# Attention's weighted values with the values as the standing operand, two heads on the two halves of the array's columns

## The reference, cut to what matters

```python
s = jnp.where(causal[None, None], s, -jnp.inf)
p = jax.nn.softmax(s, axis=-1).astype(v.dtype)
return jnp.einsum('bhqk,bkhd->bqhd', p, v)
...
o = o.transpose(1, 0, 2, 3, 4).reshape(B, S, N_HEADS * V_HEAD_DIM)
return o @ w_o
```

## Time and profile before

| what | value |
|---|---|
| median of three runs | 783.43 us (783.41 to 783.67) |
| span of the profiled execution | 780.1 us |
| lies around the span, by the median | 3.3 us |
| PE busy | 773.0 us, 99% of the span |
| DVE busy | 577.1 us, 74% |
| ACT busy | 423.9 us, 54% |
| POOL busy | 97.7 us, 13% |
| the chain that ended last | 98% PE |
| granted clock of TensorE, mean | 0.998 |

### The profile page before, as it was taken

How to read it: one execution, slowest core, us unless ns; L and a number is a source line. 1 busy time by engine, 2 the same in 40 slices (tenths; PEclk the granted TensorE clock), 3 DMA queues, 4 the chain that set the end, 5 groups by cost and what they waited for, 6 DMA issues and landing times.

```text
span 780.1 us, 10183 instructions
## 1 busy us (share of the span) xinstructions
PE 773.0 (99%) x3678; PEld 652.6 (84%) x3678; DVE 577.1 (74%) x843; ACT 423.9 (54%) x601; POOL 97.7 (13%) x147
## 2 busy tenths in 40 slices
PE   9999999999999999999999999999999999999997
PEld 7998888888888888888889888888888888888885
DVE  6699999889675566655476999998877765457543
ACT  6577555664554355454475765564536544536441
POOL 2634000221300000000211240002304000000000
PEclk9999999999999999999999999999999999999999
DMA  9687545556566666676455784456564766667741
GB/s 356 239 287 227 192 162 158 194 164 199 182 237 217 210 198 223 217 238 210 128 199 169 247 270 162 134 173 206 174 227 139 250 218 220 204 195 228 237 137 54
DMA packets 60080, 157.54 MB, mean 202 GB/s; under 512 B 11024, under 2 KB 22288, under 8 KB 60032
## 3 DMA queue, kind: packets, MB, share of 16 engines
q1 hardware_dynamic: 58480, 152.87, 59.6%
q0 software_dynamic: 1408, 3.52, 1.6%
q10 hardware_dynamic: 144, 0.52, 0.2%
HBM read 145.34 MB, written 2.62 MB: 190 GB/s over the span
## 4 chain that ended last, share of the span: by engine, by line
PE 98%; DMA 1%; DVE 0%; DVEq 0%; POOLq 0%; ACT 0%; issue 0%; POOL 0%; ACTq 0%
PE acc L528 28%; PE acc L530 28%; PE acc L529 28%; PE acc L627 7%; PE tp L602 2%; PE misc L818 1%; PE tp L836 1%; PE tp L614 1%; DMA gates<-x_cols 1%; PE tp L800 0%; PE misc L530 0%; PE misc L528 0%; PE misc L529 0%; PE misc L785 0%; PE misc L787 0%; DVE gates L1311 0%
## 5 line engine op out<-in xcount | busy, mean ns | idle before, releaser
L1291 DVE TENSOR_TENSOR w_lo<-raw,w_hi 128x1024 fp32r<-128x1024 f32 (+2 forms) x245 | 297.7, 1226 | 116.8 <-ACT w_hi L948 116.0
L948 ACT ACTIVATE w_hi<-raw 128x1024 fp32r<-128x1024 f32 (+2 forms) x251 | 257.1, 1039 | 157.4 <-PE acc L530 148.9
L528 PE MATMUL acc<-w_hi,xT_hi 128*128 128x512 f32 (+2 forms) x692 | 267.8, 387 | 0.0
L530 PE MATMUL acc<-w_hi,xT_lo 128*128 128x512 f32 (+2 forms) x692 | 264.9, 383 | 0.0
L529 PE MATMUL acc<-w_lo,xT_hi 128*128 128x512 f32 (+2 forms) x692 | 264.5, 382 | 0.0
L530 PEld LDWEIGHTS acc<-w_hi,xT_lo 128*128 128x128 f32 x692 | 129.9, 188 | 25.1
L528 PEld LDWEIGHTS acc<-w_hi,xT_hi 128*128 128x128 f32 x692 | 130.0, 188 | 23.9
L529 PEld LDWEIGHTS acc<-w_lo,xT_hi 128*128 128x128 f32 x692 | 130.0, 188 | 23.7
L528 PE MATMUL acc<-w_hi,hT_hi 128*128 128x512 f32 (+1 forms) x300 | 117.1, 390 | 0.0
L530 PE MATMUL acc<-w_hi,hT_lo 128*128 128x512 f32 (+1 forms) x300 | 116.2, 387 | 0.0
L529 PE MATMUL acc<-w_lo,hT_hi 128*128 128x512 f32 (+1 forms) x300 | 116.1, 387 | 0.0
(11 more groups left out here) (159 smaller groups left out, 641.1 us busy)
## 6 DMA issues: line engine op xcount, KB each, us to landing
raw<-weights SPq DMA_DIRECT2D x247, 512.0 KB, 4.0
raw<-weights SPq DMA_DIRECT2D x14, 384.0 KB, 3.5
gates<-gates SPq DMA_DIRECT2D x160, 32.0 KB, 2.5
raw<-weights SPq DMA_DIRECT2D x8, 288.0 KB, 4.1
gain<-gains SPq DMA_DIRECT2D x4, 512.0 KB, 6.8
qk<-gates POOLq DMA_DIRECT2D x18, 64.0 KB, 3.5
x_sb<-x_rows SPq DMA_DIRECT2D x2, 512.0 KB, 9.3
out_rows<-x_sb SPq DMA_DIRECT2D x4, 256.0 KB, 2.0
```

The source lines that it names most:

```text
L528: pe.matmul(out, a_hi, b_hi, start=start, stop=False)
L530: return pe.matmul(out, a_lo, b_hi, start=False, stop=stop)
L948: ins = act.activation(w_hi[:, s, first:end], raw[:, s, first:end], ACT.Copy, scale=by)
L1291: ins = dve.tensor_tensor(w_lo[:, s, 0:width], raw[:, s, 0:width], f(w_hi[:, s, 0:width]), ALU.subtract)
```

## The change

The probabilities are divided by their sums before they are transposed: DVE's reciprocal moves forward, to the turn after the exponentials, and in the same turn ACT multiplies the probabilities in place (`share_out`). PE's transposes wait for that. The weighted values are made once for a pair of heads, after its second half: the values (128 keys by 64) stand in the array, the transposed probabilities move through it, 256 columns for the first block of keys and 128 for the second, and the two heads write to partitions 0 to 63 and 64 to 127 of one bank, each on its half of the array's columns. The result comes out transposed, as the projection wants it, so ACT and DVE make its high and low part straight from PSUM (`hi_T`, `lo_T`) in the turn in which PE made it. The division, the turning, the moves through memory and `hi_o` and `lo_o` are gone.

```diff
-       "MT0", "MT1", *(f"{piece}{n}" for n in range(8) for piece in "PV"),
+       "MT0", "MT1", "P0", "P1", "P2", "V0", "P3", "P4", "V1", "P5", "P6", "V2", "P7", "V3",
...
-HI_OF = [n for n in TP if n[:2] != "HC" and n[0] not in "PV"]
+HI_OF = [n for n in TP if n[:2] != "HC" and n[0] != "P"]
...
-        pT = qk_flat[:, 1024:2048].rearrange("p (b i n) -> p b i n", b=2, i=4)
-        o_sb = qk_flat[:, 2048:3072].rearrange("p (t n) -> p t n", t=TOK)
+        pT = qk_flat[:, 1024:2560].rearrange("p (b i n) -> p b i n", b=2, i=2)
...
-                    for half, after in enumerate((U_GATE + 22, U_ATTNO + 1)):
-                        n = 2 * l + half + 1
-                        if u == after:
-                            blocks_out(between_o[half], turned_o[half], o_turned, TOK * n, o_out)
-                        if u == after + 2:
-                            blocks_in(between_o[half], placed_o[half], o_out, n, o_in)
...
                 def p_transposes(n):
                     t = n % 2
-                    pe.wait_ge(exp_done, l * STEPS + (n + 1))
+                    pe.wait_ge(shared_out, l * STEPS + (n + 1))
                     transposes(TPN[f"P{n}"], [(probs[:, n % 2, i, k * P:(k + 1) * P], P)
                                               for i in range(2) for k in range(t + 1)])
...
-                def weighted_values(n):
-                    hp, t = n // 2, n % 2
-                    tp_emptied(pe, l, TPN[f"P{n}"])
-                    b = TPN[f"V{n}"] % 2
-                    tp_wait(TPN[f"V{n}"])
-                    for i in range(2):
-                        h = 2 * hp + i
-                        for k in range(t + 1):
-                            mm = pe.matmul(tp[:, b, i * VDIM:(i + 1) * VDIM],
-                                           pT[:, n % 2, i * (t + 1) + k, :],
-                                           v_sb[:, k, h * VDIM:(h + 1) * VDIM], start=k == 0, stop=k == t)
+                def weighted_values(hp):
+                    for n in (2 * hp, 2 * hp + 1):
+                        tp_emptied(pe, l, TPN[f"P{n}"])
+                    b = TPN[f"V{hp}"] % 2
+                    tp_wait(TPN[f"V{hp}"])
+                    for k in range(TOK):
+                        for i in range(2):
+                            h = 2 * hp + i
+                            own = slice(i * VDIM, (i + 1) * VDIM)
+                            mm = pe.matmul(tp[own, b, k * P:SEQ], v_sb[:, k, h * VDIM:(h + 1) * VDIM],
+                                           pT[:, hp % 2, i, k * SEQ:SEQ + k * P], start=k == 0, stop=k == 1,
+                                           skip_group_check=True)
                     mm.then_inc(tp_full[b], 1)
...
-                    if v_n is not None:
-                        weighted_values(v_n)
+                    if v_n is not None and v_n % 2:
+                        weighted_values(v_n // 2)
...
-                    pe.wait_ge(o_lo, TOK * (2 * l + i + 1))
+                    for hp in (2 * i, 2 * i + 1):
+                        tp_emptied(pe, l, TPN[f"V{hp}"])
...
+                def share_out(n):
+                    keys = (n % 2 + 1) * P
+                    act.wait_ge(inv_done, l * STEPS + (n + 1))
+                    for i in range(2):
+                        p = probs[:, n % 2, i, 0:keys]
+                        e = act.activation(p, p, ACT.Copy, scale=rinv[:, n % 2, i:i + 1])
+                    e.then_inc(shared_out, 1)
                 def store_p(m):
-                    n = TPN[f"P{m}"]
+                    n, hp, t = TPN[f"P{m}"], m // 2, m % 2
                     tp_filled(act, l, n)
-                    if m >= 2:
-                        tp_filled(act, l, TPN[f"V{m - 2}"])
-                    blocks = 2 * (m % 2 + 1)
-                    act.activation(pT[:, m % 2, 0:blocks, :], split3(tp[:, n % 2, 0:blocks * P], blocks),
+                    if hp >= 2:
+                        tp_filled(act, l, TPN[f"V{hp - 2}"])
+                    keys = (t + 1) * P
+                    act.activation(pT[:, hp % 2, :, t * P:t * P + keys], split3(tp[:, n % 2, 0:2 * keys], 2),
                                    ACT.Copy).then_inc(tp_free[n % 2], 1)
-                def hi_o(half):
-                    act.wait_ge(o_in, 16 * QUADS * (2 * l + half + 1))
-                    for t in range(TOK):
-                        act.activation(o_part(hT_hi, half, t), o_placed(half, t), ACT.Copy).then_inc(o_hi, 1)
...
-                    s_n, p_n, _ = after_gate(i)
+                    s_n, p_n, v_n = after_gate(i)
                     if p_n is not None:
                         store_p(p_n)
                     if s_n is not None:
                         exponentials(s_n)
-                    if i == O_PARTS:
-                        hi_o(0)
+                    if i % 2 and after_gate(i - 1)[0] is not None:
+                        share_out(after_gate(i - 1)[0])
+                    if v_n is not None and v_n % 2:
+                        k = H_O + v_n // 2
+                        hi_T(f"V{v_n // 2}", hT_hi[:, k:k + 1, :])
...
-                his(53, 54)
-                hi_o(1)
-                his(54, 56)
+                his(53, 56)
...
-                def divide(m):
-                    hp, t = m // 2, m % 2
-                    n = TPN[f"V{m}"]
-                    tp_filled(dve, l, n)
-                    dve.wait_ge(inv_done, l * STEPS + (m + 1))
-                    dve.tensor_tensor(split3(o_sb[:, t, 2 * hp * VDIM:2 * (hp + 1) * VDIM], 2),
-                                      split3(tp[:, n % 2, 0:2 * VDIM], 2),
-                                      rinv[:, m % 2, :].unsqueeze(2).to_broadcast((P, 2, VDIM)),
-                                      ALU.mult).then_inc(tp_free[n % 2], 1)
...
                 for i in range(GATES):
                     s_n, p_n, v_n = after_gate(i)
                     if s_n is not None:
                         maxima(s_n)
-                    if p_n is not None:
-                        invert(p_n)
-                    if v_n is not None:
-                        divide(v_n)
-                    if v_n in O_TURNED:
-                        turn_o(O_TURNED.index(v_n))
+                    if i % 2 and after_gate(i - 1)[0] is not None:
+                        invert(after_gate(i - 1)[0])
+                    if v_n is not None and v_n % 2:
+                        k = H_O + v_n // 2
+                        lo_T(f"V{v_n // 2}", hT_lo[:, k:k + 1, :], hT_hi[:, k:k + 1, :])
                     if i == MEAN_AFTER + 1:
                         conv_centre()
                     lo(U_GATE + 4 + i)
...
-                    if i == O_PARTS:
-                        lo_o(0)
                     taps(4 if i < 10 else 5)
...
                 los(53, 54)
-                lo_o(1)
                 conv_var()
```

More of the change, by code:

```diff
@@ L131, in after_gate @@
     return tuple(n if 0 <= n < STEPS else None for n in range(i // 2 - 1, i // 2 - 4, -1))
-O_TURNED, O_PARTS = (3, 7), 18
 MT_AFTER, MEAN_AFTER = 2, 22
@@ L212, in build @@
         placed_q = [qk_flat[:, 512 * i:512 * (i + 1)] for i in range(QUADS - 1)] + [gates[:, 1, 512:1024]]
-        turned_o = sg[:, 0, :], qk_flat[:, 1024:1536]
-        placed_o = sg[:, 1, :], qk_flat[:, 0:512]
         turned_r, placed_r = u_sb[:, 0, :], u_sb[:, 1, :]
@@ L300, in build @@
         k_in = [sem(f"k_in{i}") for i in range(2)]
[L301 to L305, removed]
         conv_dve = sem("conv_dve")
@@ L321, in build @@
         inv_done = sem("inv_done")
+        shared_out = sem("shared_out")
         summed = sem("summed")
@@ L324, in build @@
         stored = sem("stored")
-        between_o = [nc.dram_tensor(f"between_o{n}", (QUADS, P, P), F32, kind="Internal").ap() for n in range(2)]
         between_r = nc.dram_tensor("between_r", (QUADS, P, TOK * KV_RANK // QUADS), F32, kind="Internal").ap()
@@ L386, in move_keys @@
                               ).then_inc(k_in[part], 16)
[L388 to L396, removed]
         def r_blocks(buf):
```

## The result

The changed kernel takes 792.57 us (median of 4 runs, 792.49 to 793.08) against 783.47 us (4 runs): a ratio of 1.0114, 95% interval 1.0101 to 1.0126, 9.1 us slower.

What follows compares the result with a forecast made beforehand. PE's work was taken to bound the kernel, with DVE also full in the gates' stage; 5.14 + 5.20 us of late transposes less 2 x 0.27 made +9.8 on 783.4, so 793.2 us, range 788.0 to 797.0.

Steps and rivals of the forecast that it cites:

- The wait, its place and its way: PE's transposes wait for ACT's division and DVE's reciprocal; step 7's start 7.25 us after its maxima, 5.14 and 5.20 us late.
- DVE's stand: DVE idles at `lo_T` until ACT's `hi_T`, behind the exponentials, is done: 1.47 us in the turn after a pair.
- The shift of the maxima: Differences earlier in DVE's full list add up, so step 7's maxima start 2.05 us later, at 133.62.
- The sum: Both layers' step 7 lateness less pair 3's two blocks, 5.14 + 5.20 - 2 x 0.27 = +9.8 us; chance 0.72.
- the 3.3 us around it are unchanged: Time outside the profiled span stays 3.3 us, so the span's +9.8 us goes onto the median 783.4 us.
- The bounds: 0.3 us a layer for hand-overs and divisions, pair 3's block 0.65 to 1.84: +7.8 to +11.4, 791.2 to 794.8 us.
- The clock: Rival: the clock falls to half speed in PE's new gaps, some 2.7 us each: 795.9 or 798.6 us; chance 0.10.
- The block: A pair's weighted values on PE cost 0.87 + 0.2 = 1.07 us against 1.34 before.
- both heads at once: Case for a pair's passes on PE: heads overlap fully on their halves, 0.65 us, instead of the 0.87 taken.
- the upper bound: A change of the array's division costs at most 0.27 us, 0.16 for pass and weight load plus 0.11; 0.1 taken.
- What PE saves is absorbed: Savings at pairs 0 to 2 are waited away at the next transposes; only pair 3's -0.27 us a layer counts.
- no wait binds: Rival: step 7's maxima-to-transposes way stays under 4.2 us, only PE's block counts: 781.2, down to 777.9 us; chance 0.07.

Runs made afterwards that it cites:

- experiment 1: The changed kernel with DVE's low part of a pair's result (`lo_T`) made one turn later, behind the reciprocal: 783.1 us, ratio 0.9991 to the kernel before.
- 2: The changed kernel with the reciprocal ahead of the taps, DVE's stand at `lo_T` left in: 788.43 us, ratio 1.006 to the kernel before.
- experiment 3: The changed kernel with both edits, reciprocal ahead of the taps and `lo_T` one turn later: 780.79 us, ratio 0.9961 to the kernel before.
- experiment 5: The changed kernel with both heads of a pair on the same half of the columns: 793.39 us, ratio 1.0123 to the kernel before.
- experiment 4: As experiment 3, but both heads of a pair write to the first half of the columns: 785.54 us, ratio 1.0023 to the kernel before.
- experiment 6: As experiment 3, with one more constant transpose between the two key blocks, two more division changes a pair: 782.7 us, ratio 0.9987 to the kernel before.

## Why the prediction was right

**The wait, its place and its way.** Right in kind and nearly in size. DVE's stand was put at 1.47 us; behind the reduction the next instruction can start 0.61 us after it did (131.75 - 131.14 in experiment 1), so DVE was free at 135.34 and stood until 136.78, 1.44 us. From step 7's maxima to its transposes 7.25 us were summed; it is 141.39 - 134.26 = 7.13, and 531.28 - 524.15 = 7.13 in layer 1. Experiments 1 and 2 show that both the stand and the filler ahead of the reciprocal carry the loss, and 3 that with both gone no wait at the transposes is left in the list.

**The shift of the maxima** looks too small in layer 0, 2.69 us (134.26 against 131.57) instead of 2.05, so that step 7 came 5.66 us late there instead of 5.14. But DVE came late to the first maxima already, those of step 0, before any stand. DVE's maxima of step 0 in both layers, before:

```profile
81.06 0.43 DVE L1517 TENSOR_TENSOR misc<-misc,const 128x256 f32<-128x256 f32 x1
...
465.20 0.43 DVE L1517 TENSOR_TENSOR misc<-misc,const 128x256 f32<-128x256 f32 x1
```

and with the change, with layer 1's step 7 behind them:

```profile
81.89 0.44 DVE L1497 TENSOR_TENSOR misc<-misc,const 128x256 f32<-128x256 f32 x1
...
471.78 0.43 DVE L1497 TENSOR_TENSOR misc<-misc,const 128x256 f32<-128x256 f32 x1
...
524.15 0.43 DVE L1497 TENSOR_TENSOR misc<-misc,const 128x256 f32<-128x256 f32 x1
```

In layer 0 that is 0.83 us, and it belongs to the execution: experiment 5 has the same order on DVE and comes to step 0 at 80.89. From step 0 to step 7 the maxima shift by 52.37 - 50.51 = 1.86 us in layer 0 and 52.37 - 50.50 = 1.87 in layer 1, so the 2.05 was 0.2 too much.

**The sum.** Followed by one matmul behind layer 0's stage (line 874 before, 849 after: 160.32 and 167.05), layer 0 costs 6.73 us, of which 5.66 is step 7's lateness. Layer 1 adds 11.48 - 6.73 = 4.75 (531.28 against 519.80; 5.20 were taken), and behind it 0.28 comes back (0.27 were taken). That is 11.2 us of span; the sum had 9.8. That the lateness of both layers together was right to 0.1 (10.41 against 10.34) is luck: without what DVE brought to step 0 it is 5.66 - 0.83 = 4.83 in layer 0 and 4.75 + 0.15 = 4.90 in layer 1 (471.78 is 6.58 behind 465.20, 0.15 less than the 6.73), each 0.3 less than was summed. With the two blocks of pair 3 taken off, that makes 9.2 us for the change itself. The rest arose in layer 0 behind step 7, 6.73 - 5.66 + 0.27 = 1.3 us: the clock, next point. The time rose less than the span, 9.1 us: the step "the 3.3 us around it are unchanged" failed. In the timed runs time and span differ by 1.8 us for the changed kernel and by 1.9 to 2.6, most often 2.1, for the one before, so the profiled execution of before was most likely a quick one, 1.2 us below the median's. The span came out 1.4 us above the sum and what lies around it 1.5 below; that these two cancelled is luck too.

The bounds were added up wrongly: they count pair 3's block from nothing, though the sum has its -0.27 a layer already. From the same terms they are +8.4 to +11.9, 791.8 to 795.3 us; the range stays as it is. And the 0.4 us that overlapping halves change in the sum is for both layers, 2 x 0.22, not for one.

**The clock.** This rival, at 0.10, came true in part. Busy time by stretch in the changed kernel, around layer 0's step 7 and around layer 1's:

```profile
139.00:141.00 2.00, 0.00 (x0) 0.00 (x0) 2.00 (x6) 0.57 (x2) 0.00 (x0) 0.98 0.74 252
141.00:143.00 2.00, 1.61 (x6) 1.52 (x7) 2.00 (x5) 1.74 (x3) 0.00 (x0) 0.50 0.25 47
143.00:145.00 2.00, 2.00 (x7) 1.56 (x7) 2.00 (x5) 1.97 (x3) 0.00 (x0) 0.67 0.59 225
...
530.00:532.00 2.00, 0.72 (x5) 0.69 (x6) 2.00 (x5) 1.68 (x3) 0.00 (x0) 1.00 0.45 178
```

The clock fell to 0.50 at the end of layer 0's gap, and step 7's transposes took 1.12 us instead of 0.65; in layer 1, behind an equal gap of 2.46 us, it didn't. The argument against, that 3.0 us without work had held full speed, proved too weak. The price, 2.7 us, was too high. The matmul of line 849 behind the stage, in both layers:

```profile
167.05 0.59 PE L849 MATMUL misc<-diag,const 128*128 128x256 f32 x2
...
555.60 0.59 PE L849 MATMUL misc<-diag,const 128*128 128x256 f32 x2
```

From step 7's transposes it is 167.05 - 141.39 = 25.66 us in layer 0 and 555.60 - 531.28 = 24.32 in layer 1, so the fall cost 1.3 us; by the work done at half speed in the rows above it is (1.61 + 1.3) / 2 = 1.5. The three other executions have spans of 790.7 to 790.8, 0.5 us below the profiled one's; how often the clock fell in them the runs don't show.

**The block.** 1.07 us were taken, with 0.87 for passes that overlap in part and 0.1 a change of division. By experiment 3 it is 0.97, made otherwise: by experiment 4 "both heads at once" (0.65) was the right case, 0.22 less than was taken, and by experiment 6 a change of division is 0.15, two of them 0.30 and 0.1 more than was taken. With 0.65 that is 0.95, so little is left over. The two misses went opposite ways. The Trainium skill, TensorEngine Tiling (Array Packing), Key Properties, says that tiles work independently, and experiment 4 agrees (0.64 us a pair). The other rule of the Trainium skill there is that a change of the tiling mode drains the engine, and experiment 6 agrees that a change has a price, 0.15 us, where the upper bound had 0.27.

**What PE saves is absorbed.** Right: with the longer blocks 3.4 us of PE's waits went, and step 7 came no later behind pair 0 (experiment 5). This is why halves that overlap fully show as nothing in the changed kernel, and why the rival "no wait binds" could be right about the block and wrong about the time.

## What to carry to other kernels

On an engine that has no idle time, an instruction that waits for another engine's answer to what this engine has just issued should stand a turn later, and a short result that others wait for belongs ahead of long filler: with the same instructions these two moves turned a ratio of 1.0114 into one of 0.9961. A saving on the busiest engine counts only behind its last wait on another engine, so look for the waits before you price the saving. And take the time around the span from executions that have both, not from one profile's span and another run's median.

## What the hardware showed beside that

- Two heads' float32 matmuls on different halves of the array's columns run at once though their passes alternate in PE's list: 0.87 us for eight passes against 1.51 on one half.
- Two more changes between the whole array and its halves, with a transpose of 0.11 us between them, made a pair's block 0.41 us longer: 0.15 us a change.
- The clock fell behind one gap of 2.46 us without work and not behind an equal one in the same execution, and held for 3.0 us behind the last matmul; so a gap's length alone doesn't tell whether it falls.
